# Gated delta net on one Trainium2 core: where the scan's hops stand among the inverse's products, when the scan's output is turned, and how many throwaway products open the experts

## What is computed

```
kb = k * beta;  A = strictly_lower(kb k^T * decay)
u, w = solve(A + I, [v * beta, kb * exp(gc)])      # a unit triangular solve, per chunk
scan over chunks:
    v_new = u - w S
    o     = (q exp(g)) S + attn v_new
    S     = S exp(g_last) + (k exp(g_last - g))^T v_new
y = (rmsnorm(o_forward + o_backward) * silu(h @ w_gate)) @ w_o
```

## Time and profile before

| | us |
|---|---|
| median of 3 runs | 2575.03 (2574.20 to 2575.14) |
| the profiled execution's own time | 2575.85 |
| its span in the profile | 2574.0 |
| PE busy in it | 2479.8 (96%) |
| DVE, ACT, POOL busy | 1023.8, 735.3, 543.7 |

### The profile page before, as it was taken

How to read it: one execution, slowest core, us unless ns; L and a number is a source line. 1 busy time by engine, 2 the same in 40 slices (tenths; PEclk the granted TensorE clock), 3 DMA queues, 4 the chain that set the end, 5 groups by cost and what they waited for, 6 DMA issues and landing times. The chain is left out here.

```text
span 2574.0 us, 40331 instructions
## 1 busy us (share of the span) xinstructions
PE 2479.8 (96%) x15613; PEld 1573.6 (61%) x15614; DVE 1023.8 (40%) x2361; ACT 735.3 (29%) x1603; POOL 543.7 (21%) x501
## 2 busy tenths in 40 slices
PE   7999999989999999999899999999999999999998
PEld 4565565555555555555676677766645449468484
DVE  2454455427667675113454454544442111010110
ACT  3454445221222220103354444544331111110110
POOL 0211111023323233331443234432100000000000
PEclk9999999989999999998999999999999999999999
DMA  8234222313333333211111010110339998685931
GB/s 263 72 83 131 74 72 74 108 49 98 110 117 98 115 113 95 57 45 57 35 35 34 18 35 18 35 34 11 98 106 321 345 346 270 209 274 161 291 111 29
DMA packets 323361, 299.02 MB, mean 116 GB/s; under 512 B 5952, under 2 KB 285632, under 8 KB 323104
## 3 DMA queue, kind: packets, MB, share of 16 engines
q1 hardware_dynamic: 318880, 281.58, 35.9%
q0 software_dynamic: 4352, 15.60, 2.5%
HBM read 281.95 MB, written 13.63 MB: 115 GB/s over the span
## 5 line engine op out<-in xcount | busy, mean ns | idle before, releaser
L1381 PE MATMUL bank<-hidden,weight_ring 128*128 128x384 f32 x704 | 238.7, 493 | 4.9 <-ACT hidden L451 4.9
L687 PE MATMUL bank<-weight_ring,hidden 128*128 128x384 f32 x672 | 236.8, 496 | 1.6 <-ACT work L861 1.3
L1530 DVE SCALAR_TENSOR_TENSOR weight_ring<-weight_ring,silu_c 128x256 f32<-128x256 f32 x308 | 213.7, 735 | 5.5
L1381 PEld LDWEIGHTS bank<-hidden,weight_ring 128*128 128x128 f32 x704 | 133.2, 192 | 93.7 <-issue 7.0
L1381 PE MATMUL bank<-weight_ring 128*128 128x384 f32 x528 | 181.1, 493 | 0.3 <-DVE work L1538 0.3
L687 PEld LDWEIGHTS bank<-weight_ring,hidden 128*128 128x128 f32 x672 | 121.5, 191 | 92.0 <-issue 15.4
L2653 PE MATMUL bank<-work 64*64 64x64 f32 x4608 | 156.9, 220 | 8.6 <-DVE weight_ring L3427 6.5
L2653 PEld LDWEIGHTS bank<-work 64*64 64x64 f32 x4608 | 145.9, 135 | 16.4 <-POOL work L3123 5.5
L1914 PE MATMUL bank<-work,weight_ring 128*128 128x224 f32 x768 | 147.7, 354 | 0.0
L1914 PEld LDWEIGHTS bank<-work,weight_ring 128*128 128x128 f32 x768 | 144.1, 190 | 1.9 <-ACT work L1989 1.6
L1381 PEld LDWEIGHTS bank<-weight_ring 128*128 128x128 f32 x528 | 99.4, 191 | 69.9 <-issue 5.9
(11 more groups left out here) (445 smaller groups left out, 4030.0 us busy)
## 6 DMA issues: line engine op xcount, KB each, us to landing
weight_ring<-in_moe_w_in SPq DMA_DIRECT2D x64, 1024.0 KB, 10.3
weight_ring<-in_ada_w SPq DMA_DIRECT2D x38, 1024.0 KB, 5.2
weight_ring<-in_ffn_w_in SPq DMA_DIRECT2D x44, 512.0 KB, 4.9
hidden<-in_moe_w_out SPq DMA_DIRECT2D x8, 2816.0 KB, 11.7
residual<-in_moe_w_out SPq DMA_DIRECT2D x8, 2816.0 KB, 16.5
work<-in_moe_w_in SPq DMA_DIRECT2D x16, 1024.0 KB, 10.7
weight_ring<-in_na_w_qkv SPq DMA_DIRECT2D x24, 512.0 KB, 9.9
weight_ring<-in_gdn_w_qkv SPq DMA_DIRECT2D x24, 512.0 KB, 4.4
```

The lines of the kernel that those rows point to most:

```text
L687: mm = nc.tensor.matmul(m.psum[6][:, 0:3 * P], m.H[:, k, t * P:(t + 1) * P], weights(u)[:, k, :], start=(k == 0), stop=(k == KD - 1))
L1381: mm = nc.tensor.matmul(bank[:, 0:HT], w[:, k, :], t[:, k, :], start=(first and k == 0), stop=(last and k == HK - 1), skip_group_check=True)
L1530: nc.vector.scalar_tensor_tensor(out=out, in0=ada_slab[:, k, :], scalar=by, in1=out, op0=ALU.mult, op1=ALU.add).then_inc(acc_ok, 1)
```

## The change

On PE, the hops of scan steps 8 to 11 are spread so that mostly two products of the inverse stand between one hop and the next; DVE's and ACT's lists follow. `sum_o`, `arg_o`, `inv_o` move on DVE behind `UF0` and `UF1`, and `square_o`, `root_o` on ACT behind the last `take_y`. `turn_out` and `out_o` take the number of the scan that they finish: a body calls them for the scan of the body before, on PE behind P1's first three products (in body 8 at the very start), on DVE as the first thing of the body. Body 8 also calls them for its own scan, as before. `x(6)` moves ahead of `left("q")`. In `experts`, 8 throwaway products are left of 14 (x16 for x28).

The diff, with twelve columns of indentation taken off:

```diff
@@ experts, tensor, line 1866 @@
-for _ in range(14):
+for _ in range(8):
     nc.tensor.matmul(B[2][:, 0:HALF], ident, const(m, C_CUMF, HALF), start=True, stop=True)
@@ delta_net, tensor, line 2601 @@
-def turn_out():
-    if not scan:
+def turn_out(scanned):
+    if scanned < 1:
         return
-    pe.wait_ge(act_scan_step, SS.before(h, "gate"))
-    pe.wait_ge(pool_scan_step, GS.before(h, "on"))
+    pe.wait_ge(act_scan_step, SS.before(scanned, "gate"))
+    pe.wait_ge(pool_scan_step, GS.before(scanned, "on"))
     for t in range(4):
         mm = nc.tensor.transpose(B[GATE][:, t * P:(t + 1) * P], otok[:, t, :], ident)
     mm.then_inc(pe_scan_step, TS.step("ot"))
...
 if not prep:
+    turn_out(h - 1)
     for s in range(STEPS):
...
     beside(units_after(STEPS - 1, 2), 60)
-    turn_out()
+    turn_out(h)
     beside(60, 64)
     return
...
 block_product("P1", 0, 3)
+turn_out(h - 1)
 tx(0)
...
 first(0, 0)
+first(0, 1)
 tx(8)
-first(0, 1)
+second(0, 0)
+second(0, 1)
 kv(8)
-second(0, 0)
+third(0, 0)
+third(0, 1)
 ks(9)
-second(0, 1)
+fourth(0, 0)
 tx(9)
-third(0, 0)
+fourth(0, 1)
 kv(9)
-third(0, 1)
+first(1, 0)
+first(1, 1)
 ks(10)
-fourth(0, 0)
+second(1, 0)
+second(1, 1)
 tx(10)
-fourth(0, 1)
+third(1, 0)
+third(1, 1)
 kv(10)
-first(1, 0)
+fourth(1, 0)
 ks(11)
-first(1, 1)
+fourth(1, 1)
 tx(11)
-second(1, 0)
-kv(11)
-second(1, 1)
-for d in range(2):
-    third(1, d)
-for d in range(2):
-    fourth(1, d)
 for d in range(2):
     first(GROUPS, d)
+kv(11)
 for d in range(2):
     pe.wait_ge(act_step, SC.after(h, f"Y{GROUPS}.{d}"))
     pe.wait_ge(dve_step, VE.after(h, f"Xc{GROUPS - 1}.{d}"))
     multiply(1 + d, Y, U, d, f"u.{d}")
-turn_out()
@@ scalar, line 3094 @@
 take_y(0, 0)
+take_y(0, 1)
 vn(8)
-take_y(0, 1)
 oa(9)
 vn(9)
+take_y(1, 0)
+take_y(1, 1)
 oa(10)
 vn(10)
-take_y(1, 0)
 oa(11)
-take_y(1, 1)
 vn(11)
+for d in range(2):
+    take_y(GROUPS, d)
 square_o()
 root_o()
-for d in range(2):
-    take_y(GROUPS, d)
@@ vector, line 3325: out_o(scanned) in the manner of turn_out(scanned) @@
...
 if not prep:
+    out_o(h - 1)
     dve.wait_ge(kept, 32)
...
+out_o(h - 1)
 st(0)
...
+x(6)
 left("q")
-x(6)
 right("q")
...
 x(8)
-st(8)
-x(9)
...
 take_a(0, 0)
 take_a(0, 1)
-st(9)
+st(8)
 take_b(0, 0)
 take_b(0, 1)
+x(9)
+take_c(0, 0)
+take_c(0, 1)
+st(9)
 x(10)
-take_c(0, 0)
-st(10)
-take_c(0, 1)
-x(11)
 take_a(1, 0)
 take_a(1, 1)
 take_b(1, 0)
-sum_o()
 take_b(1, 1)
+st(10)
 take_c(1, 0)
-arg_o()
+x(11)
 take_c(1, 1)
-inv_o()
 for d in range(2):
...
     less(UF, 1 + d, d, f"UF{d}")
-out_o()
+sum_o()
+arg_o()
+inv_o()
```

More of the change, by code:

```diff
@@ L3323, in inv_o, with out_o @@
                         nc.vector.reciprocal(rstd_o, rstd_o).then_inc(dve_scan_step, VS.step("inv_o"))
-                def out_o():
-                    if not scan:
+                def out_o(scanned):
+                    if scanned < 1:
                         return
-                    dve.wait_ge(pe_scan_step, TS.before(h, "ot"))
-                    turned, gates, to = (a.rearrange("p (t s n) -> p t s n", t=4, s=2) for a in (B[GATE][:, :], gate, m.O[:, h - 1, :]))
+                    dve.wait_ge(pe_scan_step, TS.before(scanned, "ot"))
+                    turned, gates, to = (a.rearrange("p (t s n) -> p t s n", t=4, s=2) for a in (B[GATE][:, :], gate, m.O[:, scanned - 1, :]))
                     for half in range(2):
@@ L3355, in body @@
                     add_group(6)
-                    out_o()
+                    out_o(h)
                     add_group(7)
                     return
+                out_o(h - 1)
                 st(0)
```

## The result

| | before | after |
|---|---|---|
| median | 2574.61 us (2572.72 to 2575.14, 4 runs) | 2597.34 us (2596.40 to 2600.08, 4 runs) |
| profiled execution's own time | 2575.85 us | 2600.08 us |
| its span | 2574.0 us | 2598.2 us |

What follows compares the result with a forecast made beforehand. PE, busy 2479.8 of 2574.0 us, was taken to bound the kernel. Terms -8.4 - 3.5 + 27.0 - 1.1 + 11 = +25.0 us on the median of 2575.0 gave 2600 us, range 2586 to 2609.

Steps and rivals of the forecast that it cites:

- part 1: Hops of steps 8 to 11 in the inverse, spread two products apart, lose waits: 1.2 us a body, -8.4 us.
- part 2: x(6) ahead of left("q") on DVE lets PE reach Q4 0.5 us earlier a body: -3.5 us.
- part 3: PE waits in turn_out for the scan's closing chain: 3.6 us in bodies 2 to 7, 5.4 in body 8, +27.0 us.
- part 4: Experts' opening: 16 throwaway instructions for 28 let PE turn the gathered rows sooner, -1.1 us.
- part 5: PE's clock falls to half behind the seven turn_out gaps, 1.6 us each: +11 us.
- The rival in which the turn is ready: At turn_out(h - 1), the closing chain ends within 2.03 us of E, so no stall: 2562 us, chance 0.08.
- The rival that the clock holds: At turn_out, the stall is there but the clock stays up: 2589 us, 2591 with one fall; chance 0.22.
- the inverse itself keeps PE full: Inverse without a scan: 24 products in 18.39 us, no gap inside, so hops together cost 5.7 us.
- the sign of success: PE's idle time ahead of Q4 (line 2729) was to go from 0.81 to about 0.3 us.
- following SP's release by 0.2 us: Experts' opening: PE's turning of the gathered rows (line 1878) was to come 0.2 us after SP's release.

Runs made afterwards that it cites:

- experiment 4: Changed kernel with turn_out moved behind ks(1) and out_o behind x(1), but hops in the order of the kernel before: 2577.56 us, 1.0010 of before.
- experiment 5: Changed kernel with the scan's hops back in their old order, the turn and its stall kept: 2611.63 us, 1.0137 of the kernel before.
- experiment 6: Kernel before with only x(6) moved ahead of left("q"): 2572.13 us, 0.9989 of before.
- experiment 3: Changed kernel with throwaway products in the wait of turn_out, 7 in bodies 2 to 7, 12 in body 8: 2583.74 us, 1.0032 of before.
- experiment 1: Changed kernel with turn_out moved on PE behind ks(1) and out_o on DVE behind x(1): 2563.98 us, 0.9956 of before.
- experiment 8: Changed kernel with its throwaway loop back at 14 (28 products): 2601.78 us, 1.0107 of the kernel before.
- experiment 2: Changed kernel with turn_out behind ks(1), out_o behind x(1), and three more output-product units ahead of kv(0) in body 8: 2559.45 us, 0.9939 of before.
- experiment 9: Changed kernel with turn_out behind ks(1), out_o behind x(1), and the throwaway loop at 14: 2564.32 us, 0.9955 of before.
- experiment 7: Kernel before with only the throwaway loop cut to 8 from 14: 2573.37 us, 0.9997 of before; on another chip 2573.19 us, 0.9993.

## Why the prediction was right, and where its terms were off

The side, the mechanism and the sum came out; three terms were mis-sized, and one thing was not foreseen. Term by term, on the spans (forecast +25.0, found +24.2):

| term | forecast | found | from |
|---|---|---|---|
| part 1, hops | -8.4 | -14.0 | 7 x (24.05 - 22.05); experiments 4 and 5 |
| part 2, `x(6)` | -3.5 | -3.0 | 7 x 0.43; experiment 6 |
| part 3, stall | +27.0 | +27.2 | 6 x 3.64 + 5.4 |
| part 4, throwaways | -1.1 | -2.5 | last line of the table of stretches |
| part 5, clock at the turns | +11 | +13.5 | 11.5 in six bodies; 2.0 in body 8, experiment 3 |
| a gap in body 7 with its clock | 0 | +3.7 | the row at 1831.22 |
| up to body 0 | 0 | -0.2 | |
| inverse of body 7 in the trace of before | 0 | -0.4 | 24.46 us, in its bodies 1 to 6 24.05 |

The found column adds up to 24.3, within rounding of the 24.2.

**Part 3** is right to 0.02 us: E + 5.67 for E + 5.65. The last tenth is luck: `sum_o` started 0.10 us earlier than taken (E + 0.59 for E + 0.69) and the chain was 0.04 us shorter (4.93 for 4.97), but PE went on 0.15 us behind the end of `scale_o`, not a few hundredths. In the main it worked because both ends of the wait were read as chains, from `UF1` to `scale_o` and from E through P1, and because DVE's list was taken strictly in order. The rival in which the turn is ready fell with it. It fell by the place of the turn alone, as experiment 1 shows.

**Part 5** is right in kind and 2.5 us too small: a short fall cost 1.69 us (experiment 3) for the 1.6 taken, but the fall of body 7 lasted 6.8 us and cost 3.1, and that of body 8 cost 2.0. The rival that the clock holds was open for good reason: one of the six equal gaps of experiment 5 left the clock up. In the changed kernel all of them fell, 6 of 6 in each of the two traces with its order. The rule of the Trainium skill, "TensorE: Matmul & The Clock Gate", Part 1, that an idle TensorE loses half its clock and regains it by sustained work, agrees with these traces but for that one gap; which gap will pay and for how long it did not tell here.

**Part 1** is the step that failed: "the inverse itself keeps PE full", so that of the hops' 5.7 us "most is their own matmuls and stays" and what can go "is 1.09 us". The gain was 2.0 us a body. The row shows no gap because a row merges instructions whose idle time between them is small. Taken apart, the starts of the 24 products of body 0 lie 0.70 us from each other six times, and 0.72 to 0.91 the other seventeen times. 24 x 0.70 = 16.8 us, where they take 18.39: the bare inverse holds 1.6 us that are not its products at their closest. So the hops cost 22.05 - 16.8 = 5.3 us over bare products, and before it was 7.3, not 5.7.

Where the 2.0 us were is read from the starts of the products in body 1 of the two traces, each hop against the same hop in the new order. `kv(8)` lost 0.36 us, just as the forecast had it. Step 11's last hop lost 0.68 where the row shows 0.52, `ks(11)` 0.33 where the row of the `first` behind it shows 0.21, and `tx(9)` 0.21 where no row shows anything; five more hops lost 0.19 together, and the products without a hop 0.2. That each of these is a wait for another engine's answer is likely by its place, but only the 0.52 us (ACT) and the 0.21 us (POOL) carry a releaser's name. The forecast had allowed for hidden waits, as in `kv(8)`, but 0.11 us of them where there were 0.9.

**Part 2** named 0.81 going to about 0.3 us ahead of `Q4` as the sign of success. The sign was wrong and the gain right within 0.1 us: the idle time grew.

**Part 4** came 1.4 us better because of a misread row. The forecast took SP's issue at 1942.98, 7.71 us behind the first throwaway product, as the time when the rows were in, and PE as 1.3 us late for it. But with 8 products PE starts 6.31 us behind the first one, and 2.03 us before SP (1968.35 and 1970.38). So the rows were in at least 1.4 us before SP's row, and before the change PE was 2.7 us late. The sign "following SP's release by 0.2 us" did not come.

**The row at 1831.22** was in no step. PE stops for 1.85 us in the middle of a product, with "issue" as the reason, which is time in which the profile shows nothing waited for; the clock falls, and the inverse of body 7 takes 3.7 us more. In the trace of experiment 8, which has the same order of instructions in that body, it stands at the same instruction, with 1.20 us and without a fall; in experiments 1 and 2 a gap of 0.32 us, in 9 one of 0.60 and in 3 one of 0.54 us stand near it, in experiment 4 and in the trace of before there is none that the timeline shows. Its cause was not tested and stays open.

The traces do point somewhere. The page of after lists a DMA queue q8 of kind "instruction" with 96 packets of 16 KB. In each body one of them lands soon after the inverse's start: in body 6 2.6 us behind it, in body 7 6.4 us, at 1829.68, and PE goes on 1.5 us later. In body 7 the weights of body 8 are under way (the DMA share is 1.15 from 1824 to 1830, and 0.02 from 1738 to 1746 in body 6). The length of the inverse of body 7 follows this landing in the other traces too. With the new order the packet lands 4.9, 5.0, 5.3 and 5.9 us behind the inverse's start in experiments 2, 1, 9 and 8, and the inverse is 0.6, 0.6, 0.9 and 1.5 us too long; in experiment 3, whose stream is longer by its throwaway products, it lands at 6.6, and a wait further on costs 0.9. With the old order a landing at 4.9 to 5.3 us (experiments 6 and 7) costs nothing, and one at 5.4 to 5.8 (4, 5, and before) 0.2 to 0.5 us. That PE ran out of instructions fits all of this. But the page doesn't say whose instructions q8 carries, and no run varied it, so it is not shown.

The misses of parts 1 and 4, -7.0 us, and those of the clock and of this gap, +6.2, nearly cancel. That the sum was within 1 us of the span is luck to that degree; the range of 2586 to 2609 held, and would have held with either group alone.

**What stays open** too: experiments 1 and 4 were both some 8 us slower than the sum of their parts. `kv(0)` accounts for 6 x 0.25 us and, by experiment 2, for some 4.5 us in body 8 (the difference of the medians and, with 109.6 - 105.2 = 4.4 us, of the traces). Another 0.4 us is the start of body 8, where `tx(0)` waits 0.66 us for `UF1` in the place that the turn had filled. The last 1.6 us were not placed; the profiled execution of experiment 1 was itself 2.3 us faster than its median, so that its trace can't show them.

## What to carry to other kernels

When work at the end of a stage is put off into the next, draw its chain from its new first operation, and put the consumer behind at least as much work as the chain is long; here a few products further down turned a loss of 22.7 us into a gain of 10. Then ask what the moved chain now stands in front of on each of the in-order engines, since that is the next wait. The waits of TensorE of 1.85 us and more in these experiments (at the turns, at `kv(0)`, at 1831.22) were paid twice with one exception, once for itself and once in the clock behind it; where such a wait can't be removed, products that compute nothing were worth putting into it. A merged row without idle time is no proof of a full engine: compare its length with the shortest distance at which its instructions start. And the time at which one engine acts is no measure of when a transfer landed for another: SP acted some 2 us behind PE on the same rows.

## What the runs showed of the hardware that was not expected

- One and the same gap of 3.46 us, behind the same products, cost 0, 1.70 or 2.63 us of clock (experiment 5), by where it fell: stretches at 1.2 GHz that began at the end of the wait or up to 1.6 us behind it lasted 3.4 us, and those that began inside it (body 7 of the changed kernel, bodies 4 to 7 in experiment 5) 6.8 us. One that began 0.1 us before the wait's end (body 6 of the changed kernel) lasted 3.4 us too.
- A gap of 2.37 us (body 8 of experiments 1, 4 and 9) and one of 1.85 us (the row at 1831.22) also let the clock fall, one of 1.20 us did not.
- The idle time that a view shows ahead of an instruction can grow while its wait shrinks, as other waits are hidden in the length of rows: `tx(6)` takes 0.82 us before and 0.43 us after for the same four instructions.
- SP and PE wait for the same gathered rows, and SP's issue stands 2.0 us behind PE's start in the changed kernel and 2.2 us in experiment 7.
- The 14 throwaway products took 9.21 us before and 8.22 in experiment 8, with the clock at 1.2 GHz for the first 5.9 and 3.9 us of them.
